# Order of the two attentions, the place of V's second buffer and of w_out, and the output norm in a one-core encoder layer

## The reference

```python
x = x + 0.5 * swiglu(rms_norm(x, ffn1_norm), ffn1_w_gu, ffn1_w_down)
proj = rms_norm(x, mix_norm) @ w_in        # conv_in, beta, a, z | dq, dk, dv
o_gdn = gated_deltanet(...)                # 4 heads of 128, blocks, state per stream
q, k = rope_partial(rms_norm(...)), ...    # 4 heads, two maps of 64 each
o_diff = (softmax1 - lam * softmax2) @ v   # prompt: causal by chunks of 64
                                           # streams: over 512 cached keys + own 16
o_diff = rms_norm(o_diff, diff_out_norm) * (1 - lam_init)   # per head
x = x + concat([o_gdn, o_diff]) @ w_out
x = x + 0.5 * swiglu(rms_norm(x, ffn2_norm), ffn2_w_gu, ffn2_w_down)
```

## Time and profile before

| | |
|---|---|
| runs of the kernel before | 1464.55, 1460.92, 1462.66 us |
| median | 1462.66 us |
| profiled execution | 1462.42 us |
| its span in the profile | 1460.6 us |
| busy in the span | PE 1373.2, PEld 1243.3, DVE 896.0, ACT 675.8, POOL 364.4 us |
| mean granted clock of PE | 0.978 of full speed |

### The profile page before, as it was taken

How to read it: one execution, slowest core, us unless ns; L and a number is a source line. 1 busy time by engine, 2 the same in 40 slices (tenths; PEclk the granted TensorE clock), 3 DMA queues, 4 the chain that set the end, 5 groups by cost and what they waited for, 6 DMA issues and landing times.

```text
span 1460.6 us, 24367 instructions
## 1 busy us (share of the span) xinstructions
PE 1373.2 (94%) x8677; PEld 1243.3 (85%) x8677; DVE 896.0 (61%) x1482; ACT 675.8 (46%) x1278; POOL 364.4 (25%) x240
## 2 busy tenths in 40 slices
PE   5999999999997999999997978789999999999999
PEld 5999999988786998787886864468999999998787
DVE  6976666644446666637456666545786667654444
ACT  5555555433334553543355532443555555543332
POOL 2555555400000000212132331000455555520000
PEclk9999999999997999999999999799999999999999
DMA  6222222270101422011021025680122222235000
GB/s 208 79 87 86 83 83 82 86 284 0 29 0 30 144 72 91 29 59 31 28 102 59 1 83 165 227 289 0 58 88 87 86 86 86 86 123 193 26 10 36
DMA packets 139254, 127.27 MB, mean 87 GB/s; under 512 B 3781, under 2 KB 107845, under 8 KB 139196
## 3 DMA queue, kind: packets, MB, share of 16 engines
q1 hardware_dynamic: 136684, 117.15, 25.1%
q0 software_dynamic: 2512, 9.34, 2.0%
HBM read 115.83 MB, written 10.39 MB: 86 GB/s over the span
## 4 chain that ended last, share of the span: by engine, by line
PE 87%; DVE 8%; ACT 2%; issue 2%; DMA 1%; POOL 0%; SPq 0%; DVEq 0%; ACTq 0%
PE psum_all L943 23%; PE psum_all L945 23%; PE psum_all L944 23%; PE psum_all L953 6%; PE psum_all L1838 2%; PE psum_all L1826 2%; PE psum_all L513 1%; PE psum_all L2104 1%; PE psum_all L1948 1%; PE psum_all L1830 1%; PE psum_all L1775 1%; DMA K_c<-cache_k 1%; PE psum_all L2246 0%; PE psum_all L2131 0%; DVE x_norm L463 0%
## 5 line engine op out<-in xcount | busy, mean ns | idle before, releaser
L943 PE MATMUL psum_all<-hw_hi,gu_op 128*128 128x320 f32 x1200 | 371.9, 310 | 2.5 <-DVE gu_op L580 2.5
L945 PE MATMUL psum_all<-hw_hi,gu_op 128*128 128x320 f32 x1200 | 372.1, 310 | 0.0
L944 PE MATMUL psum_all<-hw_lo,gu_op 128*128 128x320 f32 x1200 | 370.6, 309 | 0.0
L943 PEld LDWEIGHTS psum_all<-hw_hi,gu_op 128*128 128x128 f32 x1200 | 226.3, 189 | 3.2 <-DVE gu_op L580 2.7
L944 PEld LDWEIGHTS psum_all<-hw_lo,gu_op 128*128 128x128 f32 x1200 | 228.1, 190 | 0.0
L945 PEld LDWEIGHTS psum_all<-hw_hi,gu_op 128*128 128x128 f32 x1200 | 225.5, 188 | 0.0
L828 POOL TENSOR_TENSOR w_sum<-raw_gu 128x512 f32<-128x512 f32 x80 | 140.9, 1761 | 226.6 <-DVE gu_op L595 222.3
L595 DVE TENSOR_TENSOR gu_op<-w_sum,gu_op 128x512 fp32r<-128x512 f32 x160 | 160.9, 1006 | 57.1 <-ACT gu_op L591 51.8
L943 PE MATMUL psum_all<-wd_hi,a_hi 128*128 128x512 f32 x440 | 171.4, 390 | 1.7 <-DVE x_tok L961 1.7
L944 PE MATMUL psum_all<-wd_lo,a_hi 128*128 128x512 f32 x440 | 171.2, 389 | 0.0
L945 PE MATMUL psum_all<-wd_hi,a_lo 128*128 128x512 f32 x440 | 171.2, 389 | 0.0
(11 more groups left out here) (360 smaller groups left out, 2484.7 us busy)
## 6 DMA issues: line engine op xcount, KB each, us to landing
raw_gu<-ffn_w_gu SPq DMA_DIRECT2D x80, 512.0 KB, 4.6
wd<-ffn_w_down SPq DMA_DIRECT2D x2, 4096.0 KB, 21.0
raw_b<-w_in SPq DMA_DIRECT2D x8, 1024.0 KB, 5.2
K_c<-cache_k SPq DMA_DIRECT2D x8, 1024.0 KB, 7.6
V_c<-cache_v SPq DMA_DIRECT2D x8, 1024.0 KB, 5.6
wd<-ffn_w_down SPq DMA_DIRECT2D x2, 3584.0 KB, 12.4
raw_cv<-w_in SPq DMA_DIRECT2D x13, 512.0 KB, 3.9
wd<-ffn_w_down SPq DMA_DIRECT2D x6, 1024.0 KB, 5.0
```

Source lines behind the costliest of these rows:

```text
L943: nc.tensor.matmul(out, lhs_hi, rhs_hi, start=start, stop=False, skip_group_check=True)
L944: nc.tensor.matmul(out, lhs_hi, rhs_lo, start=False, stop=False, skip_group_check=True)
L945: return nc.tensor.matmul(out, lhs_lo, rhs_hi, start=False, stop=stop, skip_group_check=True)
```

## The change

The attention over the caches comes ahead of the prompt's in the list. V's second buffer lies in the finished halves of delta tiles 0 to 3 (`tok`, the key and value parts) and is loaded in two pieces; it waits for `o_mm` of tiles 0 and 1. Both halves of `w_out` are loaded by SP, the first after the caches' attention into memory of the K and V buffers, the second in two pieces, and POOL only loads x back. The output norm of the attention is done tile by tile beside the prompt's turns: tile 4 (the streams) first, then 0, 1, 2, and tile 3 in the output product. The turned z tiles go to other PSUM banks, `q_tok`'s are turned one step later, the splits' order changes, and SP waits for the twelfth split before it loads the first feed-forward weights. The decays of the streams (`gls`) and `gates` (22 slots in place of 20) change places.

```diff
-        V_c = a2.put("V_c", [P, 4, BANK])
-        V_c = [V_c, nc.alloc_sbuf_tensor_at("V_c1", [P, 4, BANK], F32, offset=v_at)]
+        V_c0 = a2.put("V_c", [P, 4, BANK])
+        def V_c(slot, k):
+            return V_c0[:, k] if slot == 0 else \
+                tok[:, k // 2, 4 + 4 * (k % 2):8 + 4 * (k % 2), :].rearrange("p h d -> p (h d)")
...
+        raw_o0 = nc.alloc_sbuf_tensor_at("raw_o0", [P, KT, BANK], F32, offset=d_at)
+        raw_o1 = [nc.alloc_sbuf_tensor_at(f"raw_o1{i}", [P, KT // 2, BANK], F32, offset=at)
+                  for i, at in enumerate((k_at, tok_at + 8192))]
...
+        OD_TILES = (0, 1, 2, 4, 3)
+        OD_AT = {t: i for i, t in enumerate(OD_TILES)}
+        SQUARED = {4: 1, 0: 2, 1: 3, 2: 4, 3: 6}
+        SUMMED = {4: 1, 0: 2, 1: 3, 2: 4, 3: 8}
+        TILE_OUT = {START[HEADS * qt + HEADS - 1] + OUT: qt for qt in range(3)}
+        ROOTS = START[11] + OUT + 3
+        def od_square(act, t):
+            act.wait_ge(N["pv_copied"], 1 if t == 4 else HEADS * (t + 1) + 1)
+            if t == 3:
+                act.wait_ge(N["od_chain"], SUMMED[4])
+            nc.scalar.activation(od_sq[:, OD_SLOT[t], :], q_tok[:, t, :], ACT.Square)\
+                .then_inc(N["od_act"], 1)
+        def od_sum(dve, t):
+            dve.wait_ge(N["od_act"], SQUARED[t])
+            link(dve, "od_chain", SUMMED[t], V.tensor_reduce(
+                gates[:, G_OD, OD_AT[t], :],
+                od_sq[:, OD_SLOT[t], :].rearrange("p (h d) -> p h d", d=P), AX.X, ALU.add))
+        def od_scale(dve, t, heads):
+            for h in heads:
+                V.scalar_tensor_tensor(q_tok[:, t, hc(h)], q_tok[:, t, hc(h)],
+                                       gates[:, G_E, OD_AT[t], h:h + 1], diff_gain[:], ALU.mult,
+                                       ALU.mult).then_inc(N["od_done"], 1)
+        def beside_act(act, turn):
+            if turn == 0:
+                od_square(act, 4)
+            elif turn - 1 in TILE_OUT:
+                od_square(act, TILE_OUT[turn - 1])
+            elif turn == ROOTS:
+                od_root(act, 0)
+        def beside_dve(dve, turn):
+            if turn == 1:
+                od_sum(dve, 4)
+            elif turn - 2 in TILE_OUT:
+                od_sum(dve, TILE_OUT[turn - 2])
+                if turn == ROOTS - 1:
+                    od_inverse(dve, 0)
+            elif turn == ROOTS + 1:
+                od_factor(dve, 0)
+            elif ROOTS + 2 <= turn < ROOTS + 10:
+                i = turn - ROOTS - 2
+                od_scale(dve, OD_TILES[i // 2], range(2 * (i % 2), 2 * (i % 2) + 2))
...
-            pe.wait_ge(N["qkT_copied"], 13)
             yield from att_turns(((TURN, transposes), (VALUES, values), (SCORES, scores)))
...
-                    sp.wait_ge(N["pv_mm"], len(UNITS))
-                sp.dma_start(V_c[b % 2][:], cv[b]).then_inc(s_V[b % 2], 16)
+                    sp.wait_ge(N["o_mm"], 4)
+                if b % 2:
+                    for t in range(2):
+                        sp.dma_start(tok[:, t, 4:12, :].rearrange("p (k h) d -> p k (h d)", h=HEADS),
+                                     cv[b][:, 2 * t:2 * t + 2]).then_inc(s_V[1], 16)
+                else:
+                    sp.dma_start(V_c0[:], cv[b]).then_inc(s_V[0], 16)
...
-            pe.wait_ge(N["pv_copied"], 16)
+            pe.wait_ge(N["qkT_copied"], 13)
             keys(0, (0, 1))
...
-            pool.wait_ge(N["spv_mm"], STREAMS - 2)
...
-            pool.dma_start(raw_o[0][:], w_out[:, :, 0:BANK]).then_inc(s_wo[0], 16)
-            pool.wait_ge(s_wo[0], 16)
...
-            sp.dma_start(raw_o[1][:], w_out[:, :, BANK:D]).then_inc(s_wo[1], 16)
+            sp.dma_start(raw_o0[:], w_out[:, :, 0:BANK]).then_inc(s_wo[0], 16)
+            sp.dma_start(raw_o1[0][:], w_out[:, 0:KT // 2, BANK:D]).then_inc(s_wo[1], 16)
+            sp.wait_ge(s_wo[1], 16)
+            sp.wait_ge(N["og_done"], TT * HEADS)
+            sp.dma_start(raw_o1[1][:], w_out[:, KT // 2:KT, BANK:D]).then_inc(s_wo[1], 16)
             sp.wait_ge(N["od_done"], TT * HEADS)
-            sp.wait_ge(N["og_done"], TT * HEADS)
             sp.dma_start(gain[:], io["ffn2_norm"].to_broadcast([P, D])).then_inc(s_gain[2], 16)
+            sp.wait_ge(N["wo_lo"], NTH_SPLIT[0, KT - 1])
-        BEHIND = {0: range(TT, TT + 3), 1: range(TT + 3, 2 * TT)}
+        BEHIND = {1: range(TT, TT + 3), 2: range(TT + 3, 2 * TT)}
...
-            return n if n < TT else TT + (n - TT) % 3
+            return (5, 6, 7, 1, 3)[n] if n < TT else TT + (n - TT) % 3
...
-        SPLITS = [(0, 0), (0, 1), (0, 2), (1, 0), (0, 3), (1, 1), (0, 4), (1, 2), (0, 5), (1, 3),
-                  (0, 6), (1, 4), (0, 7), (1, 5), (1, 6), (1, 7)]
+        SPLITS = [(0, 0), (0, 1), (0, 2), (0, 3), (0, 4), (1, 0), (1, 1), (0, 5), (1, 2), (0, 6),
+                  (1, 3), (0, 7), (1, 4), (1, 5), (1, 6), (1, 7)]
...
         def wout_act(act):
+            od_square(act, 3)
...
                     if k == 2:
-                        finish(diff_out_act(act, 1))
+                        od_root(act, 1)
...
         def wout_dve(dve):
+            od_sum(dve, 3)
+            od_inverse(dve, 1)
...
                     if k == 2:
-                        finish(diff_out_dve(dve, 1))
+                        od_factor(dve, 1)
+                        od_scale(dve, 3, range(HEADS))
...
         def attention_steps(eng, groups, heads, cache, prompt):
             yield from groups(eng)
             yield from heads(eng)
+            yield from cache(eng)
             yield from prompt(eng)
-            yield from cache(eng)
...
             yield from out(eng)
-            yield from diff_out(eng, 0)
```

More of the change, by code:

```diff
@@ L978, in build @@
         head_par = small.put("head_par", [P, 2, HEADS])
-        gates = small.put("gates", [P, 20, TT, HEADS])
+        gates = small.put("gates", [P, 22, TT, HEADS])
         ba = small.put("ba", [P, TT, 8])
@@ L1044, in build @@
         q_bd = a1.put("q_bd", [P, STREAMS, HEADS, 32])
+        kt_at = a1.at
         KTc = a1.put("KTc", [P, HEADS, PAST])
@@ L1487, in build @@
         (G_BETA, G_G, G_CUM, G_TOT, G_EC, G_ER, G_ET, G_RQ, G_RK, G_KB, G_KBG, G_KD, G_QD, G_A,
-         G_B, G_C, G_D, G_SSQ, G_SSK, G_E) = range(20)
+         G_B, G_C, G_D, G_SSQ, G_SSK, G_E, G_OD, G_OV) = range(22)
         gt = lambda i: gates[:, i]
@@ L2077, in build, with att_turns @@
         (SCORES, MAXIMUM, PROBS, COMBINE, TURN, TURNED, VALUES, OUT) = (0, 1, 2, 3, 5, 6, 7, 8)
-        def att_turns(stages):
+        def att_turns(stages, beside=lambda turn: None):
             for turn in range(START[-1] + OUT + 1):
@@ L2084, in att_turns @@
                         do(AT_TURN[turn - stage])
+                beside(turn)
                 yield
+        OD_TILES = (0, 1, 2, 4, 3)
+        OD_AT = {t: i for i, t in enumerate(OD_TILES)}
+        SQUARED = {4: 1, 0: 2, 1: 3, 2: 4, 3: 6}
+        SUMMED = {4: 1, 0: 2, 1: 3, 2: 4, 3: 8}
+        OD_SLOT = {4: 0, 0: 1, 1: 2, 2: 3, 3: 0}
+        TILE_OUT = {START[HEADS * qt + HEADS - 1] + OUT: qt for qt in range(3)}
[6 more added lines that the diff above has]
+                .then_inc(N["od_act"], 1)
@@ new lines, in od_sum, with od_inverse @@
+        def od_sum(dve, t):
[3 more added lines that the diff above has]
+                od_sq[:, OD_SLOT[t], :].rearrange("p (h d) -> p h d", d=P), AX.X, ALU.add))
+        OD_PART = (slice(0, 4), slice(4, 5))
+        def od_inverse(dve, part):
+            g, n = (lambda i: gates[:, i, OD_PART[part]]), (4, 8)[part]
+            link(dve, "od_chain", n + 1, V.tensor_scalar(g(G_OV), g(G_OD), 1.0 / P, EPS, ALU.mult,
+                                                         ALU.add))
+            V.reciprocal(g(G_SSK), g(G_OV)).then_inc(N["od_chain"], 1)
@@ new lines, in od_root, with od_factor @@
+        def od_root(act, part):
+            act.wait_ge(N["od_chain"], (6, 10)[part])
+            nc.scalar.activation(gates[:, G_SSQ, OD_PART[part]], gates[:, G_SSK, OD_PART[part]],
+                                 ACT.Sqrt).then_inc(N["od_act"], 1)
+        def od_factor(dve, part):
+            g = lambda i: gates[:, i, OD_PART[part]]
+            dve.wait_ge(N["od_act"], (5, 7)[part])
+            link(dve, "od_chain", (7, 11)[part], V.tensor_scalar(g(G_E), g(G_SSQ), 1.0 - LAM_INIT,
+                                                                 None, ALU.mult))
@@ L2162, in combine @@
                                        ALU.mult, ALU.add).then_inc(N["pcomb"], 1)
-            yield from att_turns(((MAXIMUM, maximum), (COMBINE, combine)))
+            yield from att_turns(((MAXIMUM, maximum), (COMBINE, combine)),
+                                 lambda turn: beside_dve(dve, turn))
         def links():
-            n, of_max, of_combine = 1, {}, {}
+            n, of_max, of_combine = 3 * STREAMS + 1, {}, {}
             for turn in range(START[-1] + OUT + 1):
@@ L2206, in out @@
```

(11 more changed lines are left out.)

99 lines of the change are left out of this document (30 added, 69 removed).

## The result

The change made the kernel slower: **1472.87 us** (median of 4 runs, 1471.97 to 1474.72) against 1462.88 for the kernel before in the same comparison. The ratio is 1.0067, 95% interval 1.0050 to 1.0084, some 10 us. I had forecast 1462.3 with a range of 1450 to 1473 and the larger part of the chances on "not slower". The profiled execution took 1472.33 us.

What follows compares the result with a forecast made beforehand. PE was taken to bound dense stretches, DVE the two heads, and neither after 866.6 us. Terms 7.8 - 2.5 + 0 - 6.3 + 0.9 = -0.1 gave 1462.3 us, range 1450 to 1473.

Steps and rivals of the forecast that it cites:

- (a) First load: Start of the caches' attention, 763.3 us: PE stands uncovered until about 767.9 for the first K, +4.7 us.
- (b) PE work in dense turns: First 44 turns, PE-bound stretches: 11 of 17 us more PE work lands here, 1.2 fills idle, +9.8 us.
- (d) clock: First 44 turns: less idle after the heads keeps PE's clock higher, -2 us (0 to -6).
- (c) Heads: Two DVE-bound stretches where a delta tile starts: work leaves DVE's queue, -1.7 and -3.0, together -4.7 us.
- Streams: Four heads of the streams' delta rule: attention leaving the loop -1.2, lower clock +1.2, sum 0 us (-3 to +6.5).
- the rest of tile 4: Delta steps after the first 44 turns, now beside two small scores: chain 6.2 us for 8.7, -2.5 us.
- Last stretch: From 908.5 to the last values: delta norm with three units 12.5, seven units alone 35, 47.5 for 53.8, -6.3 us.
- the norm in the ring: Output norm between the last units' maxima: 1.6 us on DVE, 0.5 showing of two table loads.
- Transition: Last values to first output product: ACT squares and DVE sums tile 3 first, +0.9 us (0.5 to 2).
- w_out, x and the feed-forward weights: Loads around the output product: earlier w_out and x worth 0, later first feed-forward weights 0 (up to +4 us).
- Three of the signs: Named for right: first 44 turns 105 to 114 us, streams' products mostly 1.98; for wrong: last units' ring over 5.
- the clock rival: TensorE at its lower level where prompt's small units stand beside the streams: +8, 1470.5 us, slower, chance 0.16.

Runs made afterwards that it cites:

- the level held later: Four versions of the changed kernel with unread matmuls in PE's streams' and last-stretch waits, early K load and late POOL scalings each absent or present: 1.0034, 0.9994, 0.9989, 0.9952.
- the pair of cut kernels: 192 of the 320 matmuls of the caches' values left out: in the changed kernel 1469.86 us (1.0037), in the kernel before 1466.11 us (1.0019).
- the first K early: Changed kernel with the first K load issued ahead of the waits for the last transposes and stored keys: 1467.85 us, ratio 1.0031.
- POOL later: Changed kernel in which POOL begins its three scalings of a delta tile only after DVE's five: 1474.02 us, ratio 1.0066.
- with both: Changed kernel with the first K load issued early and POOL's scalings put behind DVE's: 1460.90 us, ratio 0.9987.
- the filling: Changed kernel with unread matmuls in PE's waits of the streams' rule (8, then 12 a head) and last stretch (75): 1468.69 us, ratio 1.0034.
- the mended pair: POOL's scalings behind DVE's plus unread matmuls: changed kernel, also with early K load, 1456.33 us (0.9952); kernel before, 52 matmuls in its last stretch, 1457.38 us (0.9961).
- the two mends: First K load issued early and POOL's scalings behind DVE's, in the changed kernel: 1460.90 us, ratio 0.9987.

## Why the prediction was wrong

*(a) First load, +4.7.* It measured 4.6. But I left the clock out: PE came back from the stall at its lower level (0.68 granted over 5.3 us), and with the load early the stretch behind it was 2.7 us shorter as well in that trace; with the level held later, the load is worth 6.6 in all. The text had this stall's clock only inside a rival (1.5).

*(b) PE work in dense turns, +9.8, and (d) clock, -2.* The dense turns grew from 69.1 to 79.5 us, +10.4, their own low levels included; the two terms together said 7.8. The work was sized right: PE is busy for 11.0 us more in the dense turns (77.43 against 66.45) and for 6.0 more in the heads (24.42 against 18.45), as forecast, and the pair of cut kernels bears the asymmetry out. The clock gave nothing back: 0.94 granted from 767.7 on against 0.93. With the first K early it is 0.97, with POOL later 0.95, with both 0.98, so it was the stall above all that kept it down, and the blocked head a little.

*(c) Heads, -4.7.* **This step failed.** They went from 34.2 to 32.9 us, -1.3. The first gave 1.3 of the 1.7. The second gave nothing of its 3.0: 17.7 us in both kernels. I had read the 3.05 us as a wait that belongs to the small operation and leaves with it. It belongs to POOL, and to whatever of that kind DVE issues next. In the changed kernel this is the scaling into XR, 3.60 us. The Trainium skill, "SBUF — State Buffer", rules for kernel authors, says that a VectorE operation in a two-port mode, "or has two SBUF inputs while the GpSimd op reads SBUF", is blocked; the trace agrees (3.60 against 0.68 with POOL later). The page has it blocked until the other operation finishes; here it was held through three of 1.04 us in a row. I had weighed only its first half, against Cm, which ran in 0.28 us since POOL began 0.8 later. For this head the prediction even had a price for the rule, 1.0; the second half would have made it 3.0.

Sum of the first 44 turns: +13.7 and not +7.8, 117.0 us and not 111.1.

*Streams, 0 and -2.5 for the rest of tile 4.* The rest of tile 4 was right: up to the first product 10.0 us where it took 12.4. Four heads: 30.3 where it took 29.5, +0.8, inside my bounds. In the kernel before, the head with the slow product was only 0.5 us longer than its neighbours, so 29.0 without it; held at 2.4 GHz by the filling the changed kernel's heads take 27.8. That makes -1.2 for the attention that left the loop, as forecast, and +2.0 for the level (2.5 now against 0.5) where I had +1.2. Since filling itself costs some 0.3 us a head, both are least values.

*Last stretch, -6.3.* It measured -2.8: 51.0 against a forecast of 47.5. The chain was right: with the waits filled it takes 47.0, the norm in the ring costs 2.1 (1.6 + 0.5 forecast), a ring of tile 2 is 3.58 (3.6). Mis-sized was one term above all, the lower clock: 1.2 forecast, 3.9 shown. That is 2.7 of the 3.5 us by which this part missed; for the other 0.8 no single cause is shown.

*Transition, +0.9*: +0.8. *w_out, x and the feed-forward weights, 0*: 0; what lies behind the first product is 493.2 us long in both kernels.

*The whole.* The forecast missed by 10.2 us of span: 3.4 in the heads, 2.6 in the dense turns with their clock, 0.9 in the streams, 3.5 in the last stretch, less 0.2 in the first load and the transition. The level of PE's clock is in three of these four. Three of the signs that I had named came out against the forecast: 117.0 us for the first 44 turns, one of four products at 1.98 us, and rings of 5.15 and 5.09. That 1472.9 lies just inside the range is no merit of the sum, as the range's upper end was taken from the clock rival.

My clock rival said 1470.5 for the same reason and was the nearest, though its sign to look for, a streams' stretch under 0.75, was the wrong one: the stretch had 0.87, and the loss was shared between four places. That the order alone balances is what the mended pair shows, within its uncertainty: 0.9952 against 0.9961. The change lost by a stall that came with it (the first K, 6.6 us) and by PE's level where work was thinned out (4.8 us by the filling). POOL's block is in both kernels (4.2 us in the kernel before, 5.9 in the changed one), so it is a gain that I had counted on and that didn't come, and not a new loss.

What stays open: why the streams' stretch and the last one fall to the lower level in some executions and not in others, when their code is the same.

## What to carry to other kernels

When an operation's length in a trace is a block by another engine, price the removal by asking which instruction stands there next; the block stays with the engine that causes it. When a stage is moved to the front, look first at what its first load waits for. And where PE stands idle between matmuls that are on the path, bound the cost of its lower level by the slow and the fast row of the same matmul times all its instances, not one of them: here matmuls that nobody reads, laid into the waits, were worth 5 us without touching the order (1.0067 to 1.0034, and 0.9987 to 0.9952 on top of the two mends).

## What the runs showed of the hardware

- Work left out can make a kernel slower: 192 matmuls fewer in the kernel before cost 2.8 us (interval 1.5 to 4.2). In its trace 20 transposes of the transition took 4.53 us in place of 2.40, but that execution lies 2.8 us under the median, so what cost the 2.8 us isn't shown.
- Unread matmuls in waits held PE at 2.4 GHz: a granted clock of 1.00 over 37.8 us in which it was 0.87, and a stretch that took 37.9 to 45.5 us in nine executions became 37.8 in four of four. In the last stretch filling gave 47.0 to 47.1 us in five of five, where it was 46.5 to 51.0 in eight without.
- A VectorE multiplication of two inputs from SBUF, 0.68 us, took 3.60 while three GpSimd operations ran, and began with the first of them, and 1.26 us where only the last of three still ran. Putting GpSimd's off by some 3 us cost 0.5 us in another wait, and gave 4.2 us in the kernel before.
- The table loads of ACT were 1.28 us each, with 0.02 us from the operation before and 0.01 us to the exponential behind, and two of them inside a ring showed with 0.5 us (5.09 against 4.59).
